# Eight raw weight buffers in the attention's branch stage, whole sums of o in HBM, and P1 and P2 ahead of P5

## The chip, the cores and the metric

The kernel runs on one core of a Trainium2 chip. The metric is the device time of one execution in microseconds. The core has TensorE (PE, matrix products), VectorE (DVE), ScalarE (ACT), GpSimd (POOL) and SyncE (SP), which here only issues transfers. Each engine works through its own instructions in order and waits on semaphores. Transfers (DMA) are issued by SyncE, ScalarE or GpSimd and run on 16 DMA engines beside them.

## The reference, cut to what matters

```python
h = rmsnorm(x, norm_g)
proj = jnp.einsum('bld,dn->bln', h, w_in)      # q, k, v, f, z_att, u, gates, z_conv, m_att, m_conv
o_att = forgetting_attention(heads(q), heads(k), heads(v), log_f)     # 16 heads of 128
y_att = jnp.einsum('blc,cd->bld', o_att * jax.nn.silu(z_att), w_att_o)
o_conv = gate_b * short_conv(gate_c * u, conv_w)
y_conv = jnp.einsum('blc,cd->bld', o_conv * jax.nn.silu(z_conv), w_conv_o)
merged = jax.nn.sigmoid(m_att) * y_att + jax.nn.sigmoid(m_conv) * y_conv
return x + jnp.einsum('bld,de->ble', merged, w_out)
```

256 tokens and 16 meta tokens, width 2048, all in float32. The change is in the product with `w_att_o` (2048 x 2048), called the attention's branch stage below; `o` is `o_att * silu(z_att)` for the 256 tokens.

## The kernel before

**Precision.** Each float32 operand is used as two parts, `hi` (rounded) and `lo` (the rest), and a product is three matmuls: hi x hi, hi x lo, lo x hi (`product`, lines 1675 to 1677). So each weight goes through four steps: SyncE loads it into `w_raw`, ScalarE rounds it to `w_hi` (`round_unit`, line 722), VectorE subtracts to get `w_lo` (`split_unit`, line 1056), TensorE uses it.

**Units and rings.** Weights come in units of 128 x 1024 float32 (512 KB), numbered through the kernel. There are 4 raw buffers (`RAW`): the load of unit c waits for the split of unit c-4. Until unit 509 `w_hi` and `w_lo` have 5 slots (`CONV_RING`), so ScalarE rounds unit c only when TensorE is through with c-5; later they have 8. The room of the other slots holds side buffers until then (`t_quads`, `os_sum`, `os_pair`, `gate_wa`). In the branch stage ScalarE and VectorE run a loop over steps n: step n handles unit U_WA+n+4, preceded by whatever else is listed for step n.

**Stages.** Convolution branch and gates; its output product; attention for 8 pairs of heads (`PAIRS`), with 12 units of q, k, v weights per pair; then the branch stage, units 450 (`U_WA`) to 493; then the output projection, units 494 (`U_OUT`) to 525, 12 matmuls each; then the last norm. The last pair's attention is finished during the first units of the branch stage.

**The branch stage.** The output's four blocks of 512 columns are `nb` 0 to 3. Blocks 0 and 1 are plain products (`n` units: 12 matmuls of 512 columns, 8 units per block). Blocks 2 and 3 are computed with seven products instead of eight, from sums of weights and sums of `o`: P1 and P2 (`a` units), P5 (`t1`), P2' and P7 (`b`), P1 resumed (`t2`), P5 resumed (`b22`). These are half units: 6 matmuls of 512 columns, though 512 KB as well. The weight sums (`t_quads`) are made by VectorE during attention, stored to HBM (`t_dram`) and loaded back as `t1`, `t2` and half of `b`. The sums of `o` (`os`, four per pair) are made after each pair in `os_sum`, rounded and split in `os_pair`, stored to HBM (`os_dram`) as hi and lo, and, for pairs 0 to 6, loaded back by GpSimd in one transfer when `h` is no longer needed, since `os` takes its place.

The order of the units is written out in `wa_order`. Position 0 is unit 450:

```
0-7: n0 x8 | a a t1 n | a a t1 n | a a t1 n | a a t1 n n | b b t2 n b22 | b n b t2 n b22 | b b t2 b22 | b b t2 b22
```

**Behind the products.** Each block is multiplied by its gate (sigmoid of a 128 x 2 x 512 tile from HBM, `load_gate` and `make_gate`), the convolution's part is added (`merge_whole`, `merge_products`, both into the one buffer `merged`), TensorE turns it with 8 transposes (`turn_m`, line 1669), ScalarE and VectorE round and split it to `m_hi`, `m_lo` (`round_m`, `split_m`). `M_TURN`, `M_ROUND`, `GATED` and `GATE_STEPS` list the positions. P1 plus P2 gives `left_c`; P5 is kept in `right_c`.

**Queues.** SyncE's list is in program order: weight loads, and beside them (`beside`) the loads and stores of `t_quads` and the stores of `os`. A wait in it holds all that follows.

## Time and profile before

| what | value |
|---|---|
| median of 3 runs | 1217.35 us (1216.52 to 1217.86) |
| the profiled execution's own time | 1215.55 us |
| its span, first to last instruction | 1213.8 us |
| TensorE busy | 1193.5 us, 98% |
| VectorE / ScalarE / GpSimd busy | 972.9 / 673.8 / 29.5 us |
| read from HBM, written | 289.18 MB, 20.46 MB |
| granted clock of TensorE | 0.997 of full speed |

Times inside the kernel count from the span's start. A matmul's end is modelled and overlaps the next one's start, so a chain of matmuls is read by the distance of their starts. In rows of the timeline the bracket gives the engine's idle time ahead of the instruction and what ended it.

### The profile page before, as it was taken

The page shows a single profiled execution, that of the slowest core. Times are in us where ns is not written, and L with a number is a line of the kernel's source. Part 1 is how long each engine was busy: PE and PEld are TensorE (multiplying, and loading weights), DVE is VectorE, ACT ScalarE, POOL GpSimd, SP SyncE. Part 2 cuts the span into 40 slices and gives each one's busy share as a digit, 9 for nine tenths or more (in the row PEclk, how much of TensorE's full clock was granted, in tenths as well). Part 3 has the DMA queues.
Part 4 walks back from the last instruction along what each step waited for, and adds up shares of the span by engine and source line. Part 5 has one row for each costly group of instructions (what it writes and reads, how often), then busy time and mean ns, then how long its engine had stood idle before and what let it go on. Part 6 is the DMA issues. An engine that isn't in the chain of part 4 may idle for free.

```text
span 1213.8 us, 18111 instructions
## 1 busy us (share of the span) xinstructions
PE 1193.5 (98%) x7228; PEld 1063.8 (88%) x7228; DVE 972.9 (80%) x1184; ACT 673.8 (56%) x891; POOL 29.5 (2%) x51
## 2 busy tenths in 40 slices
PE   8999999999999999999999999999999999998997
PEld 8998898898888989889888899999999999776886
DVE  6989989989989989989955457877787777757754
ACT  7566556656556565656555435544554554655543
POOL 1000000000000000000000010000000000000000
PEclk9999999999999999999999999999999999999999
DMA  6798898897898898897677776778777887987683
GB/s 214 250 296 278 267 299 262 273 307 246 278 292 288 265 304 269 284 312 260 193 231 251 228 232 211 208 244 274 232 215 234 261 255 222 354 278 255 224 273 124
DMA packets 188739, 310.83 MB, mean 256 GB/s; under 512 B 9872, under 2 KB 128736, under 8 KB 187232
## 3 DMA queue, kind: packets, MB, share of 16 engines
q1 hardware_dynamic: 178336, 290.23, 74.0%
q10 hardware_dynamic: 9408, 15.78, 4.2%
q0 software_dynamic: 912, 3.67, 0.8%
q8 instruction: 57, 0.93, 0.3%
q14 instruction: 26, 0.21, 0.0%
HBM read 289.18 MB, written 20.46 MB: 255 GB/s over the span
## 4 chain that ended last, share of the span: by engine, by line
PE 77%; DVE 13%; DMA 6%; ACT 2%; issue 2%; ACTq 0%; POOLq 0%; POOL 0%; SPq 0%; DVEq 0%
PE ps L1675 19%; PE ps L1677 19%; PE ps L1676 19%; PE ps L1691 7%; PE ps L1690 6%; PE ps L1692 3%; PE ps L1689 3%; DMA w_raw<-t_dram 2%; DVE w_lo L1174 2%; DMA w_raw<-in_w_att_o 2%; DVE w_lo L1211 2%; DVE w_lo L1208 2%; DVE w_lo L1056 1%; DVE quads L1190 1%; DVE quads L1192 1%
## 5 line engine op out<-in xcount | busy, mean ns | idle before, releaser
L1056 DVE TENSOR_TENSOR w_lo<-w_raw,w_hi 128x1024 fp32r<-128x1024 f32 x208 | 256.4, 1239 | 129.1 <-ACT w_hi L722 128.2
L722 ACT CAST w_hi<-w_raw 128x1024 fp32r<-128x1024 f32 x210 | 219.9, 1053 | 208.1 <-PE ps L1677 113.0
L1675 PE MATMUL ps<-h,w_hi 128*128 128x258 f32 (+1 forms) x1024 | 293.6, 287 | 1.3 <-DVE w_lo L1174 1.0
L1676 PE MATMUL ps<-h,w_hi 128*128 128x258 f32 (+1 forms) x1024 | 291.2, 284 | 0.0
L1677 PE MATMUL ps<-h,w_lo 128*128 128x258 f32 (+1 forms) x1024 | 291.0, 284 | 0.0
L1675 PEld LDWEIGHTS ps<-h,w_hi 128*128 128x128 f32 x1024 | 192.7, 188 | 5.2 <-issue 1.8
L1676 PEld LDWEIGHTS ps<-h,w_hi 128*128 128x128 f32 x1024 | 192.9, 188 | 2.1
L1677 PEld LDWEIGHTS ps<-h,w_lo 128*128 128x128 f32 x1024 | 192.8, 188 | 0.0
L1174 DVE TENSOR_TENSOR w_lo<-w_raw,w_hi 128x1024 fp32r<-128x1024 f32 x122 | 148.7, 1219 | 16.0 <-ACT w_hi L778 15.8
L1691 PE MATMUL ps<-h,w_hi 128*128 128x512 f32 x408 | 159.9, 397 | 0.9 <-DVE w_lo L1174 0.9
L778 ACT CAST w_hi<-w_raw 128x1024 fp32r<-128x1024 f32 x122 | 127.4, 1053 | 28.8 <-PE ps L1677 25.0
L1690 PE MATMUL ps<-h,w_hi 128*128 128x512 f32 x360 | 142.5, 396 | 0.0
L1692 PE MATMUL ps<-h,w_lo 128*128 128x256 f32 x408 | 113.4, 278 | 0.0
L794 ACT CAST w_hi<-quads 128x1024 fp32r<-128x1024 f32 x48 | 50.7, 1057 | 110.0 <-DVE quads L1190 104.5
L1689 PE MATMUL ps<-h,w_lo 128*128 128x256 f32 x360 | 100.3, 279 | 0.0
L1692 PEld LDWEIGHTS ps<-h,w_lo 128*128 128x128 f32 x408 | 76.8, 188 | 14.7
L1675 PE MATMUL ps<-w_hi,o 128*128 128x512 f32 x216 | 85.0, 393 | 2.7 <-DVE w_lo L1056 1.5
L1677 PE MATMUL ps<-w_hi,o 128*128 128x512 f32 x216 | 84.2, 390 | 0.0
L1676 PE MATMUL ps<-w_lo,o 128*128 128x512 f32 x216 | 84.1, 390 | 0.0
L1691 PEld LDWEIGHTS ps<-h,w_hi 128*128 128x128 f32 x408 | 77.3, 190 | 6.0 <-DVE w_lo L1174 2.2
L1689 PEld LDWEIGHTS ps<-h,w_lo 128*128 128x128 f32 x360 | 67.6, 188 | 16.4
L1675 PE MATMUL ps<-w_hi,s_hi 128*128 128x512 f32 x192 | 75.1, 391 | 0.0
(241 smaller groups left out, 2124.0 us busy)
## 6 DMA issues: line engine op xcount, KB each, us to landing
w_raw<-in_w_in SPq DMA_DIRECT2D x226, 512.0 KB, 4.9
quads<-in_w_in SPq DMA_DIRECT2D x144, 512.0 KB, 4.4
w_raw<-in_w_conv_o SPq DMA_DIRECT2D x32, 512.0 KB, 4.8
w_raw<-in_w_out SPq DMA_DIRECT2D x32, 512.0 KB, 5.2
w_raw<-in_w_att_o SPq DMA_DIRECT2D x28, 512.0 KB, 5.1
quads<-in_w_in SPq DMA_DIRECT2D x48, 256.0 KB, 4.6
t_quads<-in_w_att_o SPq DMA_DIRECT2D x8, 1024.0 KB, 6.0
t_dram<-t_quads SPq DMA_DIRECT2D x8, 1024.0 KB, 9.6
```

The lines of the kernel that those rows point to most:

```text
L722: nc.scalar.copy(w_hi[:, hi_slot(c), :], w_raw[:, c % RAW, :]).then_inc(w_rounded, 1)
L778: nc.scalar.copy(w_hi[:, hi_slot(c), :], w_raw[:, n % RAW, :]).then_inc(w_rounded, 1)
L794: nc.scalar.copy(w_hi[:, hi_slot(c), :], quads[:, q, 0, :]).then_inc(w_rounded, 1)
L1056: nc.vector.tensor_tensor(w_lo[:, lo_slot(c), :], w_raw[:, c % RAW, :], w_hi[:, hi_slot(c), :].bitcast(F32), ALU.subtract).then_inc(w_spli ...
L1174: nc.vector.tensor_tensor(w_lo[:, lo_slot(c), :], w_raw[:, n % RAW, :], w_hi[:, hi_slot(c), :].bitcast(F32), ALU.subtract).then_inc(w_spli ...
L1675: nc.tensor.matmul(dst, a_hi, b_hi, start=start, stop=False, skip_group_check=resumed)
L1676: nc.tensor.matmul(dst, a_hi, b_lo, start=False, stop=False, skip_group_check=resumed)
L1677: return nc.tensor.matmul(dst, a_lo, b_hi, start=False, stop=stop, skip_group_check=resumed)
L1689: nc.tensor.matmul(dst[:, HI, :], a_lo, b[:, HI, :], start=False, stop=False)
L1690: return nc.tensor.matmul(dst, a_hi, b, start=False, stop=stop)
L1691: nc.tensor.matmul(dst, a_hi, b, start=start, stop=False)
L1692: return nc.tensor.matmul(dst[:, HI, :], a_lo, b[:, HI, :], start=False, stop=stop)
```

## The change

For units 460 to 499 (`U_RAW` to `U_LESS`, 40 units) there are 8 raw buffers: the 4 of `w_raw` and 4 more (`w_more`) in the place of `t_quads`. A load in that range waits for the split of the unit 8 before it; the first one also waits for all stores of weight sums. For the last pair all four weight sums are made at step 7 and stored after the load at position 4.

The gates of the branch stage no longer have a buffer each; they alternate between `gate_even` (0, 2) and `gate_nat` (1, 3), and are loaded at steps 3, 7, 12 and 34 (before: 3, 7, 11, 15), the last two once the buffer is free.

The sums of `o` are stored whole (float32, half the bytes) straight from `os_sum`, and loaded back by SyncE after the load at position 8, once attention's last unit is used and the last store has landed. They are rounded and split after their return, one of the four sums for all pairs at a time, at steps 9, 11, 13 and 15; `os_pair` and its copy and subtraction per pair are gone. The last pair's sums are written into the same tile.

The order of the branch stage puts all `a` units ahead of the `t1` units, and turns, roundings and merges move by a position:

```
0-7: n0 x8 | a a n | a a n | a a n | a a n | t1 t1 n | t1 t1 n | b b n t2 b22 | b n b t2 b22 | b b t2 b22 | b b t2 b22
```

The first `t1` is now at position 20 (before 10), the first `b` at 26 (before 25).

The diff, cut to its core:

```diff
-    first, second = [], []
+    first = [("a", step) for step in range(STEPS)] + [("t1", two) for two in range(STEPS // 2)]
+    second = []
     for two in range(STEPS // 2):
-        first += [("a", 2 * two), ("a", 2 * two + 1), ("t1", two)]
         second += [("b", 2 * two), ("b", 2 * two + 1), ("t2", two), ("b22", two)]
...
+MORE_RAW = 4
+U_RAW = (U_WA + 8 + RAW - 1) // RAW * RAW
+MORE_UNITS = (U_OUT + 10 - U_RAW) // (RAW + MORE_RAW) * (RAW + MORE_RAW)
+U_LESS = U_RAW + MORE_UNITS
...
-    os_pair = nc.alloc_sbuf_tensor_at("os_pair", [P, 2, 4, P], F32R, offset=spare_at + 4 * UNIT * 4 + 4 * P * 4)
-    gate_wa = nc.alloc_sbuf_tensor_at("gate_wa", [P, NB, 2, HALF], F32, offset=spare_at)
+    w_more = nc.alloc_sbuf_tensor_at("w_more", [P, MORE_RAW, UNIT], F32, offset=spare_at)
+    gate_even = nc.alloc_sbuf_tensor_at("gate_even", [P, 2, HALF], F32, offset=spare_at + 4 * UNIT * 4 + 4 * P * 4)
...
-        GATE_STEPS = (3, 7, 11, 15)
+        GATE_STEPS = (3, 7, 12, RIGHT_END + 2)
+        OS_STEPS = (9, 11, 13, 15)
...
-        M_TURN = (LEFT_END + 3, RIGHT_END + 4, N_WA + 2, N_WA + 4)
-        M_ROUND = (LEFT_END + 4, RIGHT_END + 5, N_WA + 3, N_WA + 5)
-        GATED = (LEFT_END + 1, RIGHT_END + 1, N_WA, N_WA + 3)
+        M_TURN = (LEFT_END + 4, RIGHT_END + 4, N_WA + 3, N_WA + 5)
+        M_ROUND = (LEFT_END + 5, RIGHT_END + 5, N_WA + 4, N_WA + 6)
+        GATED = (LEFT_END + 1, RIGHT_END + 1, N_WA, N_WA + 4)
...
+        def raw_unit(c):
+
+            n = (c - U_RAW) % (RAW + MORE_RAW)
+            return w_more[:, n, :] if U_RAW <= c < U_LESS and n < MORE_RAW else w_raw[:, c % RAW, :]
+
+        def raw_free(c):
+
+            return c + 1 - (MORE_RAW if U_RAW <= c < U_LESS else 0)
...
-                sp.wait_ge(w_split, count(i, per, c + 1))
-                dst = w_raw[:, c % RAW, :].rearrange("p (k n) -> p k n", k=k)
-                sp.dma_start(dst, src).then_inc(w_landed[c % RAW], 16)
+                sp.wait_ge(w_split, raw_free(c))
+                if c == U_RAW:
+                    for b in range(2):
+                        sp.wait_ge(t_stored[b], STEPS // 2 * 16)
+                sp.dma_start(raw_unit(c).rearrange("p (k n) -> p k n", k=k), src).then_inc(landed(c)[0], 16)
...
-                sp.wait_ge(os_split, i + 1)
-                sp.dma_start(os_dram[i], os_pair[:].bitcast(F32).rearrange("p s n t -> p (s n t)")
-                             ).then_inc(os_stored, 16)
+                sp.wait_ge(os_made, 4 * (i + 1))
+                sp.dma_start(os_dram[i], os_sum[:].rearrange("p n t -> p (n t)")).then_inc(os_stored, 16)
+
+            def load_os():
+
+                sp.wait_ge(w_used, RING + U_WA)
+                sp.wait_ge(os_stored, (PAIRS - 1) * 16)
+                sp.dma_start(os_x[:, 0:PAIRS - 1, :, :].rearrange("p i n t -> p i (n t)"),
+                             os_dram.rearrange("i p x -> p i x")).then_inc(os_landed, 16)
...
-                if j == 8 and 0 <= i - 1 < PAIRS:
+                if j == (8 if i < PAIRS else 4) and 0 <= i - 1 < PAIRS:
                     store_t(i - 1)
+                if n == U_WA - U_ATT + 8:
+                    load_os()
...
                     if n == step:
-                        load_gate(1, nb, gate_wa[:, nb, :, :])
+                        if nb == 1:
+                            act.wait_ge(pv_done, PAIRS)
+                        if nb > 1:
+                            act.wait_ge(free[nat_bank(nb)], FREE_A["wa"] + 1)
+                        load_gate(1, nb, gate_of(nb)[:])
                     if n == step + GATE_STEP - 2:
-                        make_gate(1, nb, gate_wa[:, nb, :, :])
+                        make_gate(1, nb, gate_of(nb)[:])
+                for part, step in enumerate(OS_STEPS):
+                    if n == step:
+                        act.wait_ge(os_landed, 16)
+                        act.wait_ge(os_made, 4 * PAIRS)
+                        nc.scalar.copy(os_hi[:, :, part, :], os_x[:, :, part, :]).then_inc(os_rounded, 1)
...
+                for part, step in enumerate(OS_STEPS):
+                    if n == step:
+                        dve.wait_ge(os_rounded, part + 1)
+                        nc.vector.tensor_tensor(os_lo[:, :, part, :], os_x[:, :, part, :],
+                                                os_hi[:, :, part, :].bitcast(F32), ALU.subtract).then_inc(os_split, 1)
...
-                    if j == 11:
+                    if j == (11 if i < PAIRS - 1 else 7):
                         sum_t(i, 2)
                         sum_t(i, 3)
...
                     elif kind == "t1":
-                        pe.wait_ge(os_landed, 16)
+                        pe.wait_ge(os_split, S1 + 1)
                     elif kind == "b":
                         pe.wait_ge(c11_summed, 1)
+                        pe.wait_ge(os_split, 4)
+                    elif kind == "b22":
                         pe.wait_ge(p_kept, 2)
```

## Rows read from the trace of the kernel before

**Rows 1.** The page: its span, the engines' busy time, and the chain by engine.
```profile
span 1213.8 us, 18111 instructions
PE 1193.5 (98%) x7228; PEld 1063.8 (88%) x7228; DVE 972.9 (80%) x1184; ACT 673.8 (56%) x891; POOL 29.5 (2%) x51
...
PE 77%; DVE 13%; DMA 6%; ACT 2%; issue 2%; ACTq 0%; POOLq 0%; POOL 0%; SPq 0%; DVEq 0%
```

**Rows 2.** Windows: length, busy us and instructions by engine, clock, DMA share, GB/s.
```profile
700.00:1044.20 344.20, 343.82 (x2485) 326.34 (x2484) 258.74 (x377) 174.23 (x292) 24.72 (x33) 1.00 0.76 241
1044.20:1116.50 72.30, 65.07 (x281) 50.42 (x280) 49.38 (x43) 43.39 (x44) 0.00 (x0) 1.00 0.85 285
1026.00:1049.00 23.00, 21.69 (x103) 17.78 (x102) 13.42 (x18) 11.32 (x16) 1.12 (x1) 1.00 1.06 388
```

**Rows 3.** Waits of TensorE, 1044.2 to 1126.5 us: total, times, longest.
```profile
PE ps L1675 <- DVE w_lo L1056: 3.6, 4, 1.2
PE ps L1669 <- DVE merged L1502: 1.6, 3, 0.6
PE ps L1675 <- DMA os<-os_dram: 1.3, 1, 1.3
PE ps L1675 <- DVE left_c L1557: 1.1, 1, 1.1
```

**Rows 4.** The chain of waits, 1034 to 1118 us: start, us, what.
```profile
1034.92 10.78 DMA w_raw<-in_w_att_o
...
1052.17 2.33 DVE w_lo L1056 x2
...
1062.50 6.54 DMA w_raw<-t_dram
...
1069.07 1.05 ACT w_hi L722
...
1070.14 1.24 DVE w_lo L1056
...
1071.44 5.75 DMA w_raw<-t_dram
```

**Rows 5.** Timeline of TensorE, 1044 to 1126 us: start, us, instruction, idle before.
```profile
1044.20 0.39 PE L1675 MATMUL ps<-w_hi,o 128*128 128x512 f32 x1
...
1045.56 0.39 PE L1675 MATMUL ps<-w_hi,o 128*128 128x512 f32 x1
...
1048.40 0.50 PE L1675 MATMUL ps<-w_hi,os 128*128 128x512 f32 x1 [1.31 <-DMA os<-os_dram]
...
1050.48 1.09 PE L1669 MATMUL ps<-ident,merged 128*128 128x128 f32 x8 [0.42 <-DVE merged L1502]
1051.33 0.48 PE L1675 MATMUL ps<-w_hi,o 128*128 128x512 f32 x1
...
1116.50 0.47 PE L1675 MATMUL ps<-w_hi,m_hi 128*128 128x512 f32 x1 [0.89 <-DVE w_lo L1056]
...
1125.46 1.09 PE L1669 MATMUL ps<-ident,merged 128*128 128x128 f32 x8 [0.56 <-DVE merged L1502]
```

**Rows 6.** Groups of instructions, 1044.2 to 1116.5 us: count, busy, mean ns, idle before.
```profile
L1056 DVE TENSOR_TENSOR w_lo<-w_raw,w_hi 128x1024 fp32r<-128x1024 f32 x35 | 42.5, 1224 | 22.5 <-ACT w_hi L722 22.0
L722 ACT CAST w_hi<-w_raw 128x1024 fp32r<-128x1024 f32 x35 | 36.6, 1053 | 28.8 <-DMA w_raw<-in_w_att_o 13.6 <-DMA w_raw<-t_dram 13.5 <-DMA w_raw<-in_w_out 1.6
```

**Rows 7.** Issues and landings: load of unit 459; `os`; gates of the stage; `t_dram`.
```profile
1024.29 0.37 SPq L542 DMA_DIRECT2D w_raw<-in_w_att_o  x1
...
1026.18 1.12 POOL L702 DMA_DIRECT2D os<-os_dram  x1 [26.91 <-DMA os_dram<-os_pair]
...
os<-os_dram POOLq DMA_DIRECT2D x1, 3584.0 KB, 22.2
...
DMA to landing us min/median/max: 5.2/7.2/9.9
...
DMA to landing us min/median/max: 4.6/6.5/13.5
```

More of the change, by code:

```diff
@@ L96, in wa_order @@
         found.append(unit)
-        if n % 3 == 2:
+        if n in (1, 3, 5, 7, 9, 11):
             found.append(next(right))
-    found.append(next(right))
     for n, unit in enumerate(second):
         found.append(unit)
-        if n in (2, 4, 6):
+        if n in (1, 4):
             found.append(next(right))
@@ L116 @@
 N_WA = len(WA_ORDER)
-A_END = max(n for n, unit in enumerate(WA_ORDER) if unit[0] in ("a", "t1"))
+A_END = max(n for n, unit in enumerate(WA_ORDER) if unit[0] == "a")
+P5_END = max(n for n, unit in enumerate(WA_ORDER) if unit[0] == "t1")
 LEFT_END = WA_ORDER.index(("n", 0, NAT_UNITS - 1))
@@ L397, in hybrid_block @@
         w_landed = [sem(f"w_landed{s}") for s in range(RAW)]
+        more_landed = [sem(f"more_landed{s}") for s in range(RAW + MORE_RAW)]
         w_rounded = sem("w_rounded")
@@ L489, in nat_bank, with gate_of @@
             return (A, B)[nb % 2]
+        def gate_of(nb):
+            return (gate_even, gate_nat)[nb % 2]
         def t_part(quad, n):
@@ L529, in f_raw, with landed @@
             return w_raw[:, landed % RAW, :].rearrange("p (k n) -> p k n", k=F_K)
+        def raw_unit(c):
+            n = (c - U_RAW) % (RAW + MORE_RAW)
+            return w_more[:, n, :] if U_RAW <= c < U_LESS and n < MORE_RAW else w_raw[:, c % RAW, :]
+        def landed(c):
+            if U_RAW <= c < U_LESS:
+                fill, n = divmod(c - U_RAW, RAW + MORE_RAW)
+                return more_landed[n], fill * 16 + 16
+            before = (HOSTED if c >= U_F else 0) + (MORE_UNITS if c >= U_LESS else 0)
+            return w_landed[c % RAW], (c - before) // RAW * 16 + 16
+        def raw_free(c):
+            return c + 1 - (MORE_RAW if U_RAW <= c < U_LESS else 0)
         def count(i, per, c):
@@ L714, in round_unit @@
             def round_unit(i, per, c):
-                landed = c - HOSTED if c >= U_F else c
-                act.wait_ge(w_landed[c % RAW], count(i, per // RAW * 16, landed // RAW * 16 + 16))
-                act.wait_ge(w_used, count(i, per, slot_reused(c)))
+                act.wait_ge(*landed(c))
+                act.wait_ge(w_used, slot_reused(c))
                 if i is None and U_F <= c < U_F + N_F:
@@ L721, in round_unit @@
                 else:
-                    nc.scalar.copy(w_hi[:, hi_slot(c), :], w_raw[:, c % RAW, :]).then_inc(w_rounded, 1)
+                    nc.scalar.copy(w_hi[:, hi_slot(c), :], raw_unit(c)).then_inc(w_rounded, 1)
             act.dma_start(meta_nat[:], meta_tokens).then_inc(meta_landed, 16)
@@ L947, in finish_pair @@
                     nc.scalar.copy(o[:, HI, i * 2:i * 2 + 2, :], prod2[:]).then_inc(o_rounded, 1)
-                if j == 8:
-                    act.wait_ge(os_made, (i + 1) * 4)
-                    if 0 < i < PAIRS - 1:
-                        act.wait_ge(os_stored, i * 16)
-                    dst = os_pair[:, HI, :, :] if i < PAIRS - 1 else os[:, i, HI, :, :]
-                    nc.scalar.copy(dst, os_sum[:]).then_inc(os_rounded, 1)
             for i in range(PAIRS):
@@ L996, in _ @@
                 c = U_WA + n + LEAD_5
-                if n <= 8:
+                if n <= 6:
                     finish_pair(PAIRS - 1, n)
-                if n == 3:
-                    for b in range(2):
-                        act.wait_ge(t_stored[b], STEPS // 2 * 16)
+                if n == GATE_STEPS[0]:
                     for part in range(4):
@@ L1055, in split_unit @@
                 else:
-                    nc.vector.tensor_tensor(w_lo[:, lo_slot(c), :], w_raw[:, c % RAW, :],
+                    nc.vector.tensor_tensor(w_lo[:, lo_slot(c), :], raw_unit(c),
                                             w_hi[:, hi_slot(c), :].bitcast(F32), ALU.subtract).then_inc(w_split, 1)
@@ L1513, in merge_whole @@
                     dve.wait_ge(os_made, 4 * PAIRS)
-                nc.vector.tensor_tensor(merged[:], ps[:, bank:bank + 2, :], gate_wa[:, nb, :, :], ALU.mult
+                nc.vector.tensor_tensor(merged[:], ps[:, bank:bank + 2, :], gate_of(nb)[:], ALU.mult
                                         ).then_inc(free[bank], 1)
@@ L1536, in merge_products @@
                     dve.wait_ge(c11_summed, 1)
-                    nc.vector.tensor_tensor(merged[:], left_c[:], gate_wa[:, nb, :, :], ALU.mult
+                    nc.vector.tensor_tensor(merged[:], left_c[:], gate_of(nb)[:], ALU.mult
                                             ).then_inc(right_made, 1)
@@ L1936, in branch_unit @@
                     elif kind == "t1":
-                        pe.wait_ge(os_landed, 16)
+                        pe.wait_ge(os_split, S1 + 1)
                     elif kind == "b":
                         pe.wait_ge(c11_summed, 1)
+                        pe.wait_ge(os_split, 4)
+                    elif kind == "b22":
                         pe.wait_ge(p_kept, 2)
-                if kind == "t1" and 2 * first + 2 == STEPS:
-                    pe.wait_ge(os_split, PAIRS)
                 pe.wait_ge(w_split, RAW + c + 1)
```

39 lines of the change are left out of this document (21 added, 18 removed).

## The prediction

> **What bounds the kernel now.** I read the page first [rows 1]: TensorE is busy 98% of the span and holds 77% of the chain that ended last, so elsewhere only less arithmetic would help. What is left to gain is idle time of TensorE on that chain. The windows say where it isn't: from 700 us to 1044.20 us TensorE is idle 0.38 of 344.2 us [rows 2]. In the 72.3 us after that, the part of the attention branch stage with the products of half a unit each, it is busy 65.07 [rows 2]. The table of its waits for 1044.2 to 1126.5 us names all of it: 3.6 us for `w_lo` from VectorE, 1.6 for `merged`, 1.3 for the transfer of `os`, 1.1 for `left_c`, 7.6 in all [rows 3].
>
> Next the question what stands behind `w_lo` and `merged`. The chain of waits for this stretch is one loop [rows 4]: a weight transfer issued at 1062.50 us takes 6.54 us, ScalarE's rounding 1.07, VectorE's split 1.24, and the split frees the raw buffer, so that the next transfer starts at 1071.44. That is 8.9 us for one turn through four buffers. TensorE needs less for four units: six matmuls start in 1.36 us (1044.20 to 1045.56 [rows 5]), so a half unit (six matmuls) is 1.36 us and an `n` unit (twelve) 2.72 us. `a, a, t1, n` is 6.8 us, `b, b, t2, b22` 5.4. So four raw buffers are too few for the transfer's delay; ScalarE stood 13.6 + 13.5 us waiting for weights in this stretch [rows 6].
>
> **How much is there.** From the first `a` unit (1044.20) to the first unit of the output projection (1116.50) are 72.30 us [rows 5]. The work in it is 28 half units and 8 `n` units, 28 x 6 + 8 x 12 = 264 matmuls at 1.36/6 = 0.2267 us, 59.85 us, and two turns of `merged` at 0.85 us (1050.48 to 1051.33 [rows 5]), 1.70: together 61.55. So 10.75 us are lost, more than the idle time that the table shows, as the first matmuls after a halt start later by some 0.2 us each. About 1.0 of that stays whatever is done: two turns are restarts too, and the matmuls on `os` run slightly slower than the others. The third turn (1125.46, 0.56 idle [rows 5], 0.7 with its restart) lies behind the stretch. Recoverable: 10.75 - 1.0 + 0.7 = 10.4 us.
>
> **The change, part by part.**
>
> *Eight raw buffers for units 460 to 499* (all of the branch stage from its position 10, and six units of the output projection). The load of a unit now waits for the split of the unit eight before it. One turn of 8.9 us now serves eight units, at least 8 x 1.36 = 10.9 us of TensorE. In terms of delay: with five `w_hi` slots a load goes out when TensorE is through with the unit thirteen before it and that much later as rounding and split take (2.3 us [rows 4]), so TensorE has twelve units of work ahead, less 4.6 us for two roundings and splits. In half units alone the transfer may take 16.3 - 4.6 = 11.7 us, in the mix with one `n` in four 15.8; before, with eight units, 6.3 and 9.0. Transfers from `t_dram` took 4.6 to 13.5 us, median 6.5 [rows 7]. This takes out the 3.6 us for `w_lo`, and the waits for `merged` and `left_c`, which are late because their engines stand in order behind a weight that has not landed (1034.92, 10.78 us, then the rounding, then `merged` [rows 4]). A rate could still bind: eight half units in 10.9 us want 8 x 0.524 MB = 4.2 MB, 385 GB/s; the DMA did 388 over 23 us [rows 2]. Over the whole stretch the demand is what was moved, 285 GB/s x 72.3 us = 20.6 MB in 61.6 us, 335 GB/s, so only the run of eleven half units from position 33 is at the edge, and its transfers are issued eight to thirteen units earlier, among `n` units. I take nothing for it, 1 us as upper bound.
>
> That row shows 388 GB/s from 1026 to 1049 us [rows 2]. The Trainium skill, "DMA: Bandwidth & Descriptors", section "Where 436 GB/s comes from", puts the limit for transfers from HBM at about 358 GB/s for one core, with 435 for the fabric. By 358 the run of half units would take 0.8 us longer per eight units, and the result would be about 1209; the measured row decides.
>
> *Whole sums of `o` to HBM, half the bytes, loaded from SyncE.* The transfer of `os` was 3.67 MB, issued by GpSimd at 1026.18 and 22.2 us on its way [rows 7]; TensorE's 1.3 us wait at 1048.40 is for it [rows 5]. Now it is 1.84 MB. Bounds: 5.2 us (the fastest 0.5 MB transfer there [rows 7]) to 22.2. I take half, 11 us: landed near 1037. It is first asked for by ScalarE at position 9, near 1045.6, and by TensorE (P5, position 20) 8 x 1.36 + 4 x 2.72 + 0.85 = 22.6 us of work after 1044.20. In SyncE's queue it sits behind the store of pair 6 and ahead of weight loads: the load of unit 459, issued at 1024.29 before [rows 7], and those of 460 to 464, which go out at once behind it. Unit 459 is needed by TensorE at 1045.56; with 2.3 us for rounding and split it may land at 1043.3, 17 us after its issue. No loss. Per pair a ScalarE copy and a VectorE subtraction go; TensorE was not waiting for either engine there [rows 2]: nothing. Instead come four casts and four subtractions of 128x1024 at positions 9, 11, 13, 15, priced like a split, 1.05 and 1.22 us [rows 6]. VectorE between positions 8 and 15 then has 8 splits, 2 for the merge, 1 for `m_lo`, 4 new: 15 operations of 1.17 (two in a row: 2.33 [rows 4]) to 1.22 us = 17.6 to 18.3 us, against 6 x 1.36 + 2 x 2.72 + 0.85 = 14.5 us of TensorE. It falls back by 3.1 to 3.8 us. Its lead is four units, 5.4 us at least, less 2.3 for rounding and split: 3.1. So 0 to 0.7 us; I take 0.3.
>
> *P1 and P2 first.* P5, the first product on `os`, moves from position 10 to 20, so the 1.3 us wait for `os` goes. `left_c` is then summed at position 19 for use at 26: the 1.1 us wait goes.
>
> *Gates through two buffers.* A gate load must now wait until the buffer's last gate was used. For the fourth the load moves from step 15 to 34 and the sigmoid to 38, with four half units, 5.4 us, between, and 3.1 us of lead behind: 8.5 us. Its transfers took 5.2 to 9.9 us, median 7.2 [rows 7]. ScalarE waits for it in order, with the roundings of positions 42 and on behind it, then VectorE's splits, then TensorE. 0 to 1.4 us; I take 0.4. At step 12 the same wait has an `n` unit more room: nothing. The wait for the last T store ahead of unit 460's load: that store moves some four units earlier (VectorE's two sums for it from step 11 to 7), so it has landed when SyncE gets there. VectorE's 14 operations over positions 33 to 43, 16.4 to 17.1 us, against 11 x 1.36 + 0.85 = 15.8 stay within the lead. *Turns one unit later*: merge 3 stands ahead of `split_m(2)` still; the last turn comes 2 units after the third, 5.4 us for a merge of 2.45: nothing, and the 0.7 of the third turn goes.
>
> Sum: 10.4 - 0.3 - 0.4 and 0.3 for what I can't see = 9.4 us. The profiled execution took 1215.55 us with a span of 1213.8; it should become 1206.1 with a span of 1204.4. It was 1.8 us under the median, so the median goes from 1217.35 to about 1208.0.
>
> **The rivals.**
>
> *The wait moves to DMA or VectorE (0.12).* Transfers get slower as more are on their way (13.5 us when `os` was among them [rows 7]), so that the DMA delivers only half of what is asked for above what it moves now: 310 GB/s, between 285 [rows 2] and the 335 wanted. The 20.6 MB then take 66.5 us, 4.9 more than 61.6. Against it: 388 GB/s in the window with most queued [rows 2]. Gain 9.4 - 4.9 = 4.5: 1212.9. VectorE's fall-back, were its lead used up already, would cost its 3.1 to 3.8 us: inside the same case.
>
> *The extra buffers don't do what they are for (0.05).* The rounding may only go five units ahead, and SyncE issues in order behind waits for `os` and the T stores; if these hold the loads back until 1044, TensorE finds the same four units and stalls the same. The gain is then the 1.3 us for `os` and what goes with it, less new waits: 1217.0. Against it: ScalarE waits for landings, not for slots, in this stretch [rows 6].
>
> *Slower: the loads queue behind `os` (0.04).* The `os` load is in the queue of the weights now. If it needed 22.2 us from 1026.2 as before, and the load of 459 behind it another 13.5 [rows 7], that landed at 1061.9, and TensorE, which wants it at 1045.56, would get it at 1064.2: 18.6 us lost, less the 9.4 gained, 1226.6. It decides from a landing later than 1043.3, and turns the sign from 1052.7. Against it: half the bytes, and a queue of hardware.
>
> **How the numbers follow.** The likeliest case has 0.79, its own range 1206.5 to 1210 (the waits above from 0 to 3.1 us, and 1 us of the recoverable time either way). 0.2% is 2.4 us, about what a measurement of this kernel can tell from no change. The range for 8 in 10 reaches up to the DMA case: 1206.0 to 1213.5. Faster takes the likeliest and nearly all of the DMA case: 0.89; within 0.2% 0.07; slower 0.04.
>
> **What would show it.** TensorE's waits in the stage: those for `w_lo`, `os`, `left_c` gone, `merged` under 0.5 us; from the first `a` unit to the first output unit 62 to 64 us; ScalarE's idle time for `w_raw` landings down from 27 us to under 5; the transfer of `os` landing within 15 us; DMA at 320 GB/s or more there. Wrong would be: a wait of TensorE for `w_lo` at positions 15 to 20 (VectorE) or 42 to 43 (fourth gate), ScalarE idle for the gate or for `os`, weights landing later than 12 us throughout, or a halt near 1045 (queue). Outside the stage nothing should move.

## The result and the profile after

The change made the kernel faster by 12.3 us: median 1205.08 us (1204.54 to 1205.8, 4 runs) against 1217.35, ratio 0.990 (0.9881 to 0.992). (A fourth run of the kernel before took 4141.51 us; with it in, the median on record is 1217.61.) The forecast was 1208.0 with a range from 1206.0: the direction and the place were right, the size too small, and the time lies 0.9 us below the range. The profiled execution took 1204.54 us with a span of 1202.6, 11.2 less than before.

The page of the changed kernel, answering to [rows 1]:

```profile
span 1202.6 us, 18102 instructions
...
PE 1190.2 (99%) x7228; PEld 1064.5 (89%) x7228; DVE 972.8 (81%) x1180; ACT 671.1 (56%) x887; POOL 27.7 (2%) x50
...
PE 87%; DVE 10%; issue 1%; ACT 1%; DMA 1%; ACTq 0%; POOLq 0%; POOL 0%; DVEq 0%
```

TensorE's busy time hardly changed; the span shrank around it, and DMA fell from 6% to 1% of the chain. The windows, answering to [rows 2]; the second goes from the first `a` unit to the first unit of the output projection:

```profile
700.00:1043.58 343.58, 343.58 (x2485) 326.31 (x2484) 256.29 (x371) 172.00 (x286) 22.88 (x32) 1.00 0.76 239
1043.58:1106.08 62.50, 62.50 (x282) 51.27 (x280) 53.80 (x48) 46.29 (x47) 0.00 (x0) 1.00 0.89 305
1026.00:1049.00 23.00, 23.00 (x108) 19.16 (x108) 17.31 (x22) 14.92 (x20) 0.00 (x0) 1.00 1.01 376
```

The stage takes 62.50 us in place of 72.30 and TensorE is busy in all of it. All waits of TensorE in the whole execution, answering to [rows 3]:

```profile
PE ps L1743 <- POOL ident L710: 1.9, 1, 1.9
PE ps L1829 <- DMA chan_rows<-in_norm_gain: 1.3, 1, 1.3
PE ps L1718 <- DVE w_lo L1210: 1.2, 3, 0.9
PE ps L1734 <- DVE w_lo L1210: 0.9, 2, 0.6
```

None lies in the branch stage; they are of the kernel's start and the convolution stage. TensorE's timeline, answering to [rows 5]:

```profile
1043.58 0.39 PE L1718 MATMUL ps<-w_hi,o 128*128 128x512 f32 x1
...
1050.38 1.03 PE L1712 MATMUL ps<-ident,merged 128*128 128x128 f32 x8
1051.17 0.47 PE L1718 MATMUL ps<-w_hi,o 128*128 128x512 f32 x1
...
1106.08 0.40 PE L1718 MATMUL ps<-w_hi,m_hi 128*128 128x512 f32 x1
...
1117.00 0.27 PE L1712 MATMUL ps<-ident,merged 128*128 128x128 f32 x1
```

The turns carry no bracket: they follow the matmul before. The third comes 10.92 us after the first output unit, four units of 2.73 us.

So the 11.2 us of the two spans are 9.8 from the stage (72.30 - 62.50), 0.7 from the third turn, and 0.6 from a stage that begins earlier (1043.58 against 1044.20; 0.38 of it is a wait for the `z` tile at 834 us that this execution did not have). The two executions' own times differ by 11.0 us (1215.55 - 1204.54). The other 1.3, up to 12.3, are in no comparison of these two traces; the first two runs below are about them.

### The profile page after: what moved, and what is told of

It reads as the page before. It is cut to its first block, busy times and chain, and to the rows that moved or that the text cites. A ratio compares the mean times of both kernels' runs of the same rounds, so it can differ in the third digit from the quotient of the medians.

```text
span 1202.6 us, 18102 instructions
## 1 busy us (share of the span) xinstructions
PE 1190.2 (99%) x7228; PEld 1064.5 (89%) x7228; DVE 972.8 (81%) x1180; ACT 671.1 (56%) x887; POOL 27.7 (2%) x50
## 4 chain that ended last, share of the span: by engine, by line
PE 87%; DVE 10%; issue 1%; ACT 1%; DMA 1%; ACTq 0%; POOLq 0%; POOL 0%; DVEq 0%
PE ps L1718 22%; PE ps L1720 22%; PE ps L1719 22%; PE ps L1734 7%; PE ps L1733 6%; PE ps L1735 3%; PE ps L1732 3%; DVE w_lo L1210 2%; DVE w_lo L1247 2%; DVE w_lo L1244 2%; DVE quads L1226 1%; DVE quads L1228 1%; DVE quads L1224 1%; DMA chan_rows<-in_norm_gain 1%; PE ps L1743 0%
## 5 line engine op out<-in xcount | busy, mean ns | idle before, releaser
L1092 DVE TENSOR_TENSOR w_lo<-w_raw,w_hi 128x1024 fp32r<-128x1024 f32 x188 | 232.3, 1243 | 107.9 <-ACT w_hi L754 107.6
L754 ACT CAST w_hi<-w_raw 128x1024 fp32r<-128x1024 f32 x190 | 198.5, 1050 | 182.1 <-PE ps L1720 113.3
L1210 DVE TENSOR_TENSOR w_lo<-w_raw,w_hi 128x1024 fp32r<-128x1024 f32 x122 | 148.8, 1220 | 15.9 <-ACT w_hi L810 15.7
L810 ACT CAST w_hi<-w_raw 128x1024 fp32r<-128x1024 f32 x122 | 127.0, 1050 | 28.3 <-PE ps L1720 25.1
L1732 PEld LDWEIGHTS ps<-h,w_lo 128*128 128x128 f32 x360 | 67.6, 188 | 16.5
```

The source lines that it names most:

```text
L754: nc.scalar.copy(w_hi[:, hi_slot(c), :], raw_unit(c)).then_inc(w_rounded, 1)
L810: nc.scalar.copy(w_hi[:, hi_slot(c), :], w_raw[:, n % RAW, :]).then_inc(w_rounded, 1)
L1092: nc.vector.tensor_tensor(w_lo[:, lo_slot(c), :], raw_unit(c), w_hi[:, hi_slot(c), :].bitcast(F32), ALU.subtract).then_inc(w_split, 1)
L1210: nc.vector.tensor_tensor(w_lo[:, lo_slot(c), :], w_raw[:, n % RAW, :], w_hi[:, hi_slot(c), :].bitcast(F32), ALU.subtract).then_inc(w_spli ...
L1732: nc.tensor.matmul(dst[:, HI, :], a_lo, b[:, HI, :], start=False, stop=False)
```

## The experiments

Each kernel was timed in rounds beside the kernel before on the same chip, so its ratio stands for itself; medians of before were 1216.2 to 1217.7. The text compares medians of different rows; where these were not timed together, up to 1.5 us can lie in that, and the ratios are given too where they say something else. "Changed" is the kernel with the whole change; the names in brackets are those that the expectations use.

| kernel | median us | ratio to before (95%) |
|---|---|---|
| before, again (e0_before) | 1217.22 | 0.9995 (0.9984 to 1.0007) |
| changed, again (e1_after) | 1205.49 | 0.9901 (0.9883 to 0.9920) |
| changed, depth 4 (e2_wait4) | 1211.04 | 0.9946 (0.9930 to 0.9963) |
| changed, depth 5 (e5_wait5) | 1204.55 | 0.9895 (0.9871 to 0.9919) |
| changed, old order (e4_oldorder) | 1208.37 | 0.9926 (0.9908 to 0.9945) |
| changed, old turns (e16_turns_old) | 1204.41 | 0.9895 (0.9879 to 0.9911) |
| before + new order (e3_order) | 1217.59 | 1.0008 (0.9995 to 1.0021) |
| before + order + turns (e11_order_turns) | 1214.72 | 0.9977 (0.9965 to 0.9989) |
| ... + earlier T store (e17_tstore) | 1212.82 | 0.9965 (0.9953 to 0.9977) |
| ... + later gates (e18_tstore_gate) | 1213.63 | 0.9977 (0.9968 to 0.9987) |
| changed, 4 more VectorE operations (e7_dve4) | 1207.37 | 0.9927 (0.9911 to 0.9942) |
| changed, last gate 3 steps later (e8_gate3) | 1206.69 | 0.9923 (0.9907 to 0.9940) |
| changed, 2.10 MB more ahead of `os` (e9_queue2) | 1210.52 | 0.9957 (0.9941 to 0.9974) |
| changed, 3.15 MB more (e10_queue3) | 1213.43 | 0.9976 (0.9965 to 0.9988) |
| depth 4, 2.10 MB more ahead of `os` (e12_wait4_queue2) | 1217.01 | 1.0005 (0.9990 to 1.0019) |
| depth 4, `os` from GpSimd (e14_wait4_pool) | 1211.08 | 0.9949 (0.9934 to 0.9964) |
| depth 4, `os` + 2.10 MB from GpSimd (e13_wait4_pool2) | 1211.91 | 0.9955 (0.9941 to 0.9970) |
| changed, `os` + 2.10 MB from GpSimd (e15_pool2) | 1205.57 | 0.9902 (0.9886 to 0.9918) |

### Before and changed, once more

No edit.

> The kernel before, unchanged, against itself. In one profiled execution the span fell by 11.2 us with the change, in the medians the time fell by 12.5. Theory: the profiled execution of before was one of the short ones, because its stage with four raw buffers hangs on the delays of single transfers and so varies by 1 to 2 us from execution to execution. Then another profiled execution shows a time from the first a unit to the first output unit of 73 to 75 us in place of 72.3, and the ratio to itself is 1.000 within 0.001. Rival: the surplus has another place; then the stage is 72 to 72.6 us again and the span differs elsewhere.

> The changed kernel, unchanged, in five rounds beside the others. Theory: 12 to 13 us faster than before (ratio 0.9893 to 0.9901), stage 62.5 us again within 0.2, since TensorE has no wait in it. Rival (the profile's difference is the true one): 11.2 us, ratio 0.9908.

The second profiled execution of before had a span of 1216.3 us. Its first and third turn, in TensorE's timeline:

```profile
1052.11 0.48 PE L1669 MATMUL ps<-ident,merged 128*128 128x128 f32 x1 [2.23 <-DVE merged L1502]
...
1127.97 0.66 PE L1669 MATMUL ps<-ident,merged 128*128 128x128 f32 x4 [2.37 <-DVE merged L1502]
```

In [rows 5] these waits were 0.42 and 0.56 us. The stage itself took 71.6 us, less than the 72.3 of the first, so the expectation of 73 to 75 was wrong; but from its first `a` unit (1045.60) to the first addition of the output (1192.8) it took 147.2 us against 146.0, as the third turn halts for 2.4 us behind the stage. Another 1.4 us came before it, nearly all in the first 40 us of the span: the first `cu` of the convolution was at 42.1 us against 40.9. The changed kernel's second execution began the stage at 1044.45 and took 62.49 us for it, the first 62.50. The 23 runs of before beside these went from 1214.48 to 1221.16 us, the five of the changed kernel from 1205.38 to 1206.86. By its traces this second pair is 12.8 us apart: 9.15 in the stage, 2.5 at the third turn, 1.15 in the earlier start. So what before loses in this region differs between the two executions, by 1.1 to 1.2 us; the spread of all runs fits that: the standard deviation is 1.8 us over the 109 runs of before in these experiments and 0.7 over the nine of the changed kernel. How much of the scatter lies in the stage two traces can't tell.

The size of the gain is less sure than 12.3 makes it look. In the rounds here the medians are 11.1 us apart (1216.61 and 1205.49) at a ratio of 0.9901 (0.9883 to 0.9920), an interval that holds both the theory's 0.9893 to 0.9901 and the rival's 0.9908. Over all 109 runs of before (median 1216.79) and the nine of the changed kernel (1205.40) it is 11.4 us. Of the expectation for the kernel before, the ratio to itself came (0.9995).

### The depth of the raw ring

```diff
-            return c + 1 - (MORE_RAW if U_RAW <= c < U_LESS else 0)
+            return c + 1                                              # depth 4
+            return c + 1 - (1 if U_RAW <= c < U_LESS else 0)          # depth 5
```

> The changed kernel with its eight raw buffers, but a load waits for the split of the unit four before it, as in the kernel before. Theory (the depth of four is what stalled TensorE): most of the gain goes, 7 to 10 us slower than the changed kernel, about 1212 to 1215, with waits of TensorE for w_lo and merged back. Rival (order, half the bytes of os, or gates made the gain): within 3 us of the changed kernel.

> The changed kernel with a depth of five instead of eight. Theory (what counts is the delay a transfer may have; one more buffer gives 1.36 us more of it, against transfers of 5 to 6 us): most of the 5.6 us between depth four and eight comes back, 1206 to 1208, at most one stall of TensorE. Rival (in proportion to the buffers, as with a shortage of rate): a quarter comes back, 1209.5 to 1210.5.

Depth four gives back 5.6 us of the gain, less than the 7 to 10 expected; depth five gives back nothing, and TensorE's table of waits is empty from 1043 to 1130 us. With depth four the stage took 67.6 us and TensorE ran without a halt until 1096; then:

```profile
1096.64 0.55 PE L1712 MATMUL ps<-ident,merged 128*128 128x128 f32 x3 [0.73 <-DVE merged L1540]
...
1106.26 0.50 PE L1718 MATMUL ps<-w_hi,o 128*128 128x512 f32 x1 [2.64 <-DVE w_lo L1092]
```

This is the run of half units, where four units are 5.4 us of work. A turn of the loop (transfer, rounding, split) took 7.6 us there from 1079.64, and the next one, with two merge operations in front of the splits on VectorE, 12.8. That a single buffer more ends it speaks for the delay that a transfer may have, not for a shortage of rate, which would have given a quarter back.

### Order, turns and the pieces around them

The new order alone on the kernel before; then with `M_TURN`, `M_ROUND`, `GATED` of the changed kernel; then with the last weight sums at step 7 and their store after the load at position 4; then with gate steps 3, 7, 12, 34.

```diff
+    first = [("a", step) for step in range(STEPS)] + [("t1", two) for two in range(STEPS // 2)]     # order
+        M_TURN = (LEFT_END + 4, RIGHT_END + 4, N_WA + 3, N_WA + 5)                                  # turns
+                if j == (8 if i < PAIRS else 4) and 0 <= i - 1 < PAIRS:                             # T store
+        GATE_STEPS = (3, 7, 12, RIGHT_END + 2)                                                      # gates
```

> The kernel before with only the new order of units (P1, P2 ahead of P5; P5 kept on its own). Theory: it takes the wait for os (1.5 us with its restart) and most of the wait for left_c (1.3) and leaves the loop through four buffers: 1 to 4 us faster than before. Rival (the order is worth nothing while loads are late, since the next unit waits for its weights instead): within 1 us of before.

> The kernel before with the new order and the turns, roundings and merges a position later. Theory (late weights hold ScalarE and VectorE, and the third turn waits 0.6 to 2.6 us for them; one more unit of 2.7 us covers that): 1 to 2.5 us faster than before, no wait at the third turn, waits for w_lo unchanged. Rival (the time only moves into the next wait for weights): within 1 us of before.

> The kernel before with the new order and turns (e11, 1214.7 us), and the last pair's weight sums made at step 7 and stored after the load at position 4, as in the changed kernel. Theory (the 1.05 MB store at 1023 us stood between the weight loads that give the stage its lead; at 1010 us the DMA has room): 1 to 3 us faster than e11, 1212 to 1213.5. Rival (the 3 us are elsewhere): within 0.7 us of e11.

> The same with the third and fourth gate loaded at steps 12 and 34 in place of 11 and 15. Theory (ScalarE and the DMA are relieved where the half units begin): 0.5 to 1.5 us faster than e17. Rival (a gate of 0.5 MB weighs nothing): within 0.7 us of e17; what is left against e2_wait4 then lies with the os sums made per pair against whole, which no run here separates.

The order alone is worth nothing: TensorE no longer waited for `os` or `left_c`, but 4.1 us for `w_lo` and 4.3 for `merged`, where it had been 3.6 and 1.6. The sum of the waits is 8.4 us in place of 7.6, as if the time had moved into the next wait. But the second execution of before, with no edit, had 2.2 and 5.2, 0.7 for `left_c` and none for `os`: which instruction pays changes from execution to execution as well. With the later turns it became 2.1 us faster, with the earlier store 1.9 more (1.5 by the ratios, whose intervals overlap); the gates gave nothing (0.8 slower by the medians, with intervals that overlap). In the profiled executions the stage took 71.3, 69.9, 68.8 and 68.0 us in this order. On the changed kernel the two pieces were taken back one at a time.

```diff
-    first = [("a", step) for step in range(STEPS)] + [("t1", two) for two in range(STEPS // 2)]
+        first += [("a", 2 * two), ("a", 2 * two + 1), ("t1", two)]                                  # old order
-        M_TURN = (LEFT_END + 4, RIGHT_END + 4, N_WA + 3, N_WA + 5)
+        M_TURN = (LEFT_END + 3, RIGHT_END + 4, N_WA + 2, N_WA + 4)                                  # old turns
```

> The changed kernel with the old order of units (t1 between the a units, the first at position 10); the first subtraction for os is at step 9. Theory (the order matters once the loads are no longer late, because P5 asks for the split sums right after they are made): VectorE finishes the first os_lo at 1048.7 us, TensorE wants it at 1046.3, so 2 to 3 us slower than the changed kernel, 1207.5 to 1208.5. Rival (order is worth nothing, as in the run with order alone): within 0.7 us of 1205.4.

> The changed kernel with the turns, roundings and merges at their old positions. Theory (the later position only covers engines that are late for want of weights, and they no longer are; merge 2 is ready at 1112.5 us in the trace, the turn would ask at 1114.3): within 0.7 us of 1205.4. Rival (the turns keep their worth, as in the run on the kernel before): 1.5 us slower or more.

The old order costs 2.9 us here by the medians. TensorE's one wait in that stage is the split of the sums, made at step 9 and asked for at position 10:

```profile
1049.84 0.50 PE L1719 MATMUL ps<-w_hi,os_hi 128*128 128x512 f32 x1 [2.28 <-DVE os_lo L1597]
...
1052.81 0.63 PE L1719 MATMUL ps<-w_hi,o 128*128 128x512 f32 x1
```

The profiled execution, the slowest of six, took 66.6 us for the stage, 4.1 more than the changed kernel. 2.5 are the halt with its restart. The other 1.6 are in no table of waits: from 1051.1 to 1054.1 us the matmuls start 0.43 us apart in place of 0.23, and the clock granted to TensorE, the third number from the end in this window, is 0.50, the lower of its two levels (1.2 and 2.4 GHz):

```profile
1051.31:1054.29 2.98, 2.98 (x8) 2.30 (x8) 2.98 (x3) 1.04 (x1) 0.00 (x0) 0.50 0.73 220
```

The old turns cost nothing once the weights come in time. So order and turns swap their worth: before, the turns mattered and the order did not; after, the order matters and the turns do not.

### VectorE's lead and the last gate

```diff
+                        nc.vector.tensor_tensor(spare, os_x[:, :, part, :],
+                                                os_hi[:, :, part, :].bitcast(F32), ALU.subtract).then_inc(extra, 1)
```

```diff
-        GATE_STEPS = (3, 7, 12, RIGHT_END + 2)
+        GATE_STEPS = (3, 7, 12, RIGHT_END + 5)
-                    if n == step + GATE_STEP - 2:
+                    if n == step + (1 if nb == NB - 1 else GATE_STEP - 2):
```

> The changed kernel with four more subtractions of 128x1024 on VectorE, one at each of steps 9, 11, 13 and 15, into tiles not in use then. By the prediction's account the lead of 3.1 us is used up already, so all 4 x 1.14 = 4.5 us would show, 1209.5 to 1210. Theory after the trace (with an n unit in every four the lead there is 4.5 us, and w_lo is ready at least 2.4 us ahead of its matmul): the first 2.4 us are free, 1.5 to 2.5 us slower, 1207 to 1208. Rival (VectorE has room throughout): within 0.7 us.

> The changed kernel with the last gate loaded at step 37 in place of 34, and made at 38 as before. Theory (ScalarE waits in order for it, and the roundings of positions 42 and on stand behind): issued near 1096.4, landed 6.2 to 8.1 us later, then 3.3 us for sigmoid, rounding and split, wanted at 1103.3: 2.5 to 4.5 us slower, 1208 to 1210. Rival (the lead or the eight buffers hide it): within 0.7 us.

Four more operations of 1.14 us cost 1.9 us by the medians. In the profile the table of TensorE's waits in the stage has one line:

```profile
PE ps L1724 <- DVE w_lo L1093: 2.3, 3, 1.5
```

That table leaves out what each restart costs. From the first `a` unit to the first output unit this execution, the slowest of six, took 65.72 us, 3.2 more than the 62.5 of the changed kernel. Of the 4.6 us added 3.2 show, so the room was 1.3 here; by the medians it would be 2.7, by the ratios (0.9927 against 0.9901, 3.2 us) again 1.4. The gate: in the profiled execution it was issued at 1095.33, landed 5 us later, and ScalarE waited 0.84 us for it; the stage still took 62.49 us. This is ScalarE's timeline there:

```profile
1095.33 0.37 ACTq L930 DMA_DIRECT2D gate_nat<-gates_dram  x1
...
1100.32 1.06 ACT L936 ACTIVATE gate_nat<-gate_nat 128x1024 f32<-128x1024 f32 x1 [0.84 <-DMA gate_nat<-gates_dram]
```

That execution was the fastest of six (1205.51 us); three others took 1207.5 to 1208.2. Their traces are not at hand, so a later landing in them is argued, not shown. The expected 2.5 to 4.5 us did not come in the median (1.2 us above the changed kernel); by the ratios (0.9923 against 0.9901) it would be 2.7, with intervals that overlap, so this run leaves the cost of the later gate open.

### More bytes in SyncE's queue

2.10 MB of weights into `os_hi` before it is made, and with 3.15 MB also into `left_c` and `right_c`; ScalarE waits for them with `os`. The same with a depth of four.

```diff
+                sp.dma_start(os_junk[:], w_att_k[:, 0:STEPS, 0:HALF]).then_inc(more_os[0], 16)
                 sp.dma_start(os_x[:, 0:PAIRS - 1, :, :].rearrange("p i n t -> p i (n t)"),
                              os_dram.rearrange("i p x -> p i x")).then_inc(os_landed, 16)
```

> The changed kernel with 2.10 MB more in SyncE's queue right ahead of the load of os, with all eight buffers. The weight of unit 459, which landed at 1036.2 us, then lands near 1041.6. By the prediction's rule (no loss until it lands at 1043.3, 1042.7 in this trace): within 0.7 us of 1205.4. Theory (ScalarE rounds in order, with the first gate's table load and sigmoid behind, so the merge and VectorE's whole run up to position 18 start some 4 us later against 2.4 us of room): 1.5 to 3 us slower, 1207 to 1208.5.

> The same with 3.15 MB more. Unit 459 lands near 1044.2. By the prediction's rule 1.5 us slower, 1207. By the theory of order on ScalarE and VectorE 4 to 5 us slower, 1209.5 to 1210.5. If the eight buffers take it up as a lead that was never used: within 1 us.

> The run with a depth of four (e2_wait4), and 2.10 MB more in SyncE's queue right ahead of the load of os (into os_hi, before it is made; ScalarE waits for it before its first cast), so that as many bytes cross at that place as in the kernel before. Theory (the 3.67 MB of os in the kernel before used up the lead of weights with which the stage starts, and a depth of four can't win it back): 3 to 6 us slower than e2_wait4, 1214 to 1217, TensorE's first stall near 1050 us in place of 1096. Rival (order or turns made the other half of the gain): within 1.5 us of e2_wait4's 1211.0.

The first two were slower than expected, the third by as much, and none in the place I had named. ScalarE, VectorE and TensorE in the first of them:

```profile
1041.10 1.04 ACT L757 CAST w_hi<-w_raw 128x1024 fp32r<-128x1024 f32 x1 [8.49 <-DMA w_raw<-in_w_att_o]
1042.05 0.61 ACT L982 CAST o<-prod 128x512 fp32r<-128x512 f32 x1
```

```profile
1042.17 1.23 DVE L1097 TENSOR_TENSOR w_lo<-w_raw,w_hi 128x1024 fp32r<-128x1024 f32 x1 [6.35 <-ACT w_hi L757]
1043.32 0.68 DVE L1443 TENSOR_TENSOR o<-prod,o 128x512 fp32r<-128x512 f32 x1
```

```profile
1044.05 0.50 PE L1723 MATMUL ps<-w_hi,o 128*128 128x512 f32 x1 [3.07 <-DVE o L1443]
```

Unit 459 is rounded at ScalarE's step 5, and the last pair's `o` at step 6. A late unit 459 therefore holds up `o`, which TensorE needs at position 7, not at 9 where the unit itself is used. From landing (1041.10) to TensorE's restart are 2.95 us (1044.05); undisturbed, position 7 starts a unit of 2.73 ahead of the first `a`, 1043.58 - 2.73 = 1040.85. So unit 459 must land by 1037.9. In the changed kernel:

```profile
1036.25 1.05 ACT L754 CAST w_hi<-w_raw 128x1024 fp32r<-128x1024 f32 x1 [3.60 <-DMA w_raw<-in_w_att_o]
1037.20 0.61 ACT L979 CAST o<-prod 128x512 fp32r<-128x512 f32 x1
```

It landed 1.6 us in time. The trace with 2.10 MB lost 3.4 us there (14.36 us from the end of the last pair's products to the first `a` unit, against 10.99); it was the fastest of six, and the median lost 5.0. With 3.15 MB more, TensorE stood 6.56 us there, ran at a granted clock of 0.53 for the next 3.0, and lost 8.2 in all; the median was 7.9 us above the changed kernel's. In both, the stage itself took 62.5 us: with eight buffers the loss stays outside it. The run with a depth of four lost 5.8 us ahead of the first `a` unit against depth four alone (from the end of the last pair's products to that unit 16.84 us against 11.00), and its first halt in the stage came at 1103. Its halt was the same as with eight buffers, 3.12 us against 3.07, but behind it the clock fell here and did not fall there; these are the windows behind the two halts, depth four and depth eight:

```profile
1044.92:1050.63 5.71, 5.71 (x13) 4.46 (x14) 3.39 (x7) 2.98 (x4) 0.00 (x0) 0.50 0.85 264
...
1044.05:1048.00 3.95, 3.95 (x17) 3.30 (x18) 3.03 (x6) 3.70 (x4) 0.00 (x0) 1.00 1.06 410
```

Thirteen matmuls took 5.71 us where 2.95 would do, so about half of the 5.8 us is the clock and not the halt. That the median of 2.10 MB at a depth of eight, 5.0 us where its trace lost 3.4, has the same reason is argued, not shown. The run at a depth of four was as slow as before by size, not by the mechanism, and so says nothing on the bytes of `os` in the kernel before.

### The bytes of os in GpSimd's queue

```diff
+            pool.wait_ge(w_used, RING + U_WA)
+            pool.wait_ge(os_stored, (PAIRS - 1) * 16)
+            nc.gpsimd.dma_start(os_junk[:], w_att_o.rearrange("(k p) n -> p k n", p=P)[:, 0:STEPS, 0:HALF]
+                                ).then_inc(more_os[0], 16)
+            nc.gpsimd.dma_start(os_x[:, 0:PAIRS - 1, :, :].rearrange("p i n t -> p i (n t)"),
+                                os_dram.rearrange("i p x -> p i x")).then_inc(os_landed, 16)
```

> The run with a depth of four (e2_wait4, 1211.0 us), its load of os issued by GpSimd as in the kernel before, and 2.10 MB more issued ahead of it there (into os_hi, before it is made), so 3.9 MB in that queue against 3.7 MB before, beside the weights and not ahead of them. Theory (those bytes delay the weight transfers from 1026 to 1048 us, and a depth of four starts the stage without a lead): 2.5 to 4.5 us slower than e2_wait4, 1213.5 to 1215.5, with stalls on w_lo before 1075. Rival (the bytes cost nothing in a queue of their own): within 1 us of 1211.

> As e2_wait4, with the load of os (1.84 MB) issued by GpSimd, nothing more. Theory (bytes count, not the queue): within 1 us of e2_wait4, 1210.5 to 1212. Rival (GpSimd's queue is slower for the rest of the traffic, or SyncE's order protected the weights): 1.5 to 4 us slower.

> The changed kernel, depth eight, with 3.9 MB in GpSimd's queue as in e13. Theory (a depth of eight takes up slow transfers): within 1 us of 1205.4, no stall in the stage. Rival (the unit 459 still lands too late for the last pair's o, as with 2.10 MB more in SyncE's queue, 1210.5): 3 us slower or more.

In e14_wait4_pool the load into `os_junk` is left out. The queue makes no difference (1211.08 against 1211.04), and twice the bytes cost 0.8 us at a depth of four, with intervals that overlap, not 2.5 to 4.5; its first halt came at 1094.8, not before 1075. At a depth of eight they cost nothing in the median, though transfers got slow. Median us to landing, 1020 to 1049 us, in that run:

```profile
w_raw<-in_w_att_o SPq DMA_DIRECT2D x7, 512.0 KB, 14.9
...
os_junk<-in_w_att_o POOLq DMA_DIRECT2D x1, 2048.0 KB, 15.4
os_x<-os_dram POOLq DMA_DIRECT2D x1, 1792.0 KB, 23.1
```

Weights into `w_raw` took 14.9 us in place of 11.4, and the stage still lasted only 63.4 us.

## Why the prediction came out too high

**What it had right.** The stage was where the time was; its waits for `w_lo`, `merged`, `os` and `left_c` all went. It forecast 62 to 64 us for the stage, and 62.50 came. The 1.0 us that stays whatever is done was right: 62.50 against the 61.55 counted. Of its marks, ScalarE's 27 us of waiting for weights in the stage is gone, and `os` landed after 11.0 us where half of 22.2 was taken. The DMA moved 305 GB/s there, 19.1 MB, not 320 or more; that the rest had been loaded ahead of the stage is argued, not shown. Its 10.4 us of recoverable time came as 10.5, stage and third turn. Neither the DMA's rate nor VectorE took the gain: the rival with 1212.9 did not come.

**The first step that failed: the 1.0 us taken off for new waits.** None came. From one profiled execution to the other the prediction forecast 9.4 us (to 1206.1), and 11.0 came (1204.54). 1.0 of the 1.6 between them is this term. 0.3 for VectorE: the lead was counted as four half units, 5.4 us, while every four units there hold an `n`, 6.8 us; less 2.3 that is 4.5, and with 15 operations at 1.14 (the distance of 1.13 to 1.14 in the trace after) against 14.5 us a fall-back of 2.6. That leaves a room of 1.9; the run with four added operations found 1.3 in its trace and 2.7 by the medians. 0.4 for the last gate: it had landed when ScalarE came to it. 0.3 for what I could not see: there was nothing. The other 0.6 is luck: the stage began that much earlier, and in the traces where nothing halts ahead of it it begins anywhere from 1043.3 to 1045.6 us, with either kernel.

**The second: from one execution to the median.** The prediction said that its execution was 1.8 us under the median and let the median fall by as much as the execution. That holds for an offset that both kernels share. The execution of before was 1.8 us under its median (1217.35), that of the changed kernel only 0.5 under its own: 1.3 us, and with the 11.0 between the two executions' own times 12.3. The loss in before does vary: its second profiled execution waited 2.4 us at the third turn where the first waited 0.6, and its granted clock was 0.50 for 3.0 us from the first turn on, which had waited 2.2. But medians of three and four runs are part of this term too. Against the medians of 109 and nine runs the two executions were 1.2 and 0.9 us under, so only 0.4 of the 1.3 stays, and 9.4 stands against 11.4: 1.0 for waits that did not come, 0.6 for the early start, 0.4 for this. Either way the forecast missed by sizes, not by the mechanism. The lower end of the range, 1206.0, is a gain of 11.35 us on 1217.35: room for the sum without new waits, but not for the early start and the smaller offset with it.

**What each part was worth.** The prediction gave nearly all to the eight buffers. Depth four against eight is 5.6 us. The rest is order, turns, store and `os`: 5.6 by the medians of the rounds in which before, depth four and the changed kernel ran together (1216.61, 1211.04, 1205.49), 6.6 by the ratio. From below, order with turns is 2.1, the earlier T store 1.5 to 1.9 (which the prediction priced at nothing). From 1212.8, or 1213.6 with the later gates, to depth four's 1211.0 some 1.8 to 2.6 us stay, of which the bytes of `os` may be 0.8; the last 1 to 2 us are open, and hardly more than these medians can tell. No run separates the sums made per pair from the whole ones. These pieces overlap: with the buffers in place the turns are worth nothing and the order 2.9, which can include the clock behind the halt.

**The rival on the slow side** had its mechanism right and its threshold wrong. It let the load of unit 459 come until 1043.3 (its 17 us count from 1026.2; from the issue that it names, 1024.29, they are 19.0); the true limit is 1037.9, as the unit stands ahead of the last pair's `o` in ScalarE's order. 1.6 us were left, and 2.10 MB more in the queue cost 5 us in the median. In that run the ratio is still 0.9957: for a result slower than before more than 3.15 MB would have to be added.

**The DMA page.** The Trainium skill, "DMA: Bandwidth & Descriptors", section "Where 436 GB/s comes from", gives about 358 GB/s for one core from HBM. The window from 1026 to 1049 us moved 376 GB/s in the changed kernel, 388 before. Those rows give a DMA share of 1.01 and 1.06, which can't be over 1, so the rates may be too high by as much: 372 and 366 GB/s are then the least. They are still above 358, though by little; the measured rate decides, and the stage at 305 GB/s was below either.

## What to carry to other kernels

A ring of buffers is deep enough when the work of the units in flight covers one transfer's delay with the rounding behind it; here a depth of four fell short by 5.6 us, and a depth of five was as good as eight. While weights come late, a better order may only move the wait to the next instruction; give the depth first and judge order and positions after. A stage that hangs on single transfers can scatter from execution to execution: profile it twice, and time both kernels more than three or four times before a miss of 1 us is explained. Add up a halt by the distance of the matmuls' starts, not by the table of waits: restarts and a lower clock behind the halt are not in the table.

When a transfer is put into a queue, look for the first thing that the engine behind it would have done next, not for the use of the delayed weight: here it was `o`, two positions earlier.

## What the runs showed of the hardware

Transfers of weights of 512 KB took 5.4 to 5.9 us at the median in the stage of the kernel before. From 1020 to 1049 us it was 10.8 there, beside 3.67 MB of `os` (medians of one tile's loads each, here and below); 11.4 and 12.1 in the changed kernel beside 1.84 MB; 14.9 and 13.1 with 3.9 MB from GpSimd, 12.2 and 11.0 with 3.9 MB from SyncE. But with a depth of four and the same 1.84 MB it was 5.0 and 6.9: how many weight loads are out counts as well as the other bytes.

The granted clock of TensorE was 1.00 in the stage of both kernels' first traces. It was 0.50, or 0.53 over the whole of such a stretch, for 3.0 to 5.7 us at once or some 1.3 us behind halts of 2.2 us (second trace of before), 2.3 (old order), 3.1 (depth four, 2.10 MB) and 6.6 (3.15 MB), and stayed at 1.00 behind others of 2.4 to 3.1 us (third turn of before's second trace, new order alone, depth four, 2.10 MB at a depth of eight). The length of the halt alone does not decide it in these traces.

A float32 subtraction of 128x1024 on VectorE shows 1.22 us, but operations in a row start 1.13 to 1.14 us apart, and it is this distance that counts in a sum.
